# Delta-rule inversion in a hybrid decoder trunk: the running product of the squaring kept in one orientation, the other made once by transposes

## The reference, cut to what matters

```
kb = k * beta[..., None]
lower = jnp.where(strict, jnp.einsum('nbhcd,nbhmd->nbhcm', kb, k) * decay, 0.0)
a_mat = lower + jnp.eye(C, dtype=q.dtype)
rhs = jnp.concatenate([v * beta[..., None], kb * jnp.exp(gc)[..., None]], axis=-1)
sol = lax.linalg.triangular_solve(a_mat, rhs, left_side=True, lower=True)
```

## Time and profile before

| | |
|---|---|
| median of 3 runs | 2170.37 us (2168.41 to 2171.08) |
| profiled execution, its own time | 2169.47 us |
| its span, first to last instruction | 2167.6 us |
| PE busy | 2016.2 us (93%) |
| DVE busy | 1561.4 us (72%) |
| ACT busy | 1083.2 us (50%) |
| mean granted TensorE clock | 0.954 |
| the squaring, layer 0 | from 258.06 to 279.76 us |
| the squaring, layer 1 | from 913.45 to 935.15 us |

### The profile page before, as it was taken

The page is one execution under the profiler, slowest core; times in us unless marked ns, Lnnn a source line. Parts: engine busy times, 40 slices in busy tenths (PEclk is TensorE's granted clock), DMA queues, the critical chain, the costliest instruction groups (busy, mean ns, idle before and its releaser), DMA issues.

```text
span 2167.6 us, 29976 instructions
## 1 busy us (share of the span) xinstructions
PE 2016.2 (93%) x11258; PEld 1676.8 (77%) x11258; DVE 1561.4 (72%) x2174; ACT 1083.2 (50%) x1307; POOL 160.9 (7%) x245
## 2 busy tenths in 40 slices
PE   5899999989998889999979999999999999999996
PEld 2676787789998667787868878787887877888784
DVE  6582735465565483734579898999989989899996
ACT  1114221155433214221148777787777777777773
POOL 3631000000001731000000000000000000000000
PEclk9899997989999989997979999999999999999998
DMA  7465414455544345414439999999989999999992
GB/s 299 146 247 206 146 40 175 140 195 181 178 156 137 108 149 178 156 33 153 162 113 350 370 343 337 325 364 361 352 324 344 365 343 357 325 349 367 343 345 103
DMA packets 143224, 523.79 MB, mean 242 GB/s; under 512 B 17136, under 2 KB 17520, under 8 KB 142320
## 3 DMA queue, kind: packets, MB, share of 16 engines
q1 hardware_dynamic: 138960, 506.56, 65.2%
q10 hardware_dynamic: 3488, 10.07, 1.2%
q0 software_dynamic: 640, 5.35, 0.7%
HBM read 515.48 MB, written 6.43 MB: 241 GB/s over the span
## 4 chain that ended last, share of the span: by engine, by line
PE 77%; DVE 12%; POOL 4%; ACT 4%; issue 2%; DMA 1%; ACTq 0%; DVEq 0%; POOLq 0%
PE bank L859 25%; PE bank L272 14%; PE bank L885 14%; PE bank L725 10%; PE bank L429 4%; DVE wlo L1983 3%; PE bank L806 1%; DVE arena L1579 1%; ACT whi L1154 1%; PE bank L846 1%; PE bank L445 1%; PE bank L699 1%; PE bank L712 1%; PE bank L394 1%; DVE sx L1306 1%
## 5 line engine op out<-in xcount | busy, mean ns | idle before, releaser
L1983 DVE TENSOR_TENSOR wlo<-ring,whi 128x1024 fp32r<-128x1024 f32 x756 | 910.2, 1222 | 165.4 <-ACT whi L1154 159.5
L1154 ACT ACTIVATE whi<-ring 128x1024 fp32r<-128x1024 f32 x756 | 800.8, 1061 | 314.7 <-PE bank L859 150.9
L272 PE MATMUL bank<-hT,ring 128*128 128x264 f32 x1408 | 334.1, 398 | 11.6 <-issue 6.5
L272 PEld LDWEIGHTS bank<-hT,ring 128*128 128x128 f32 x1408 | 274.5, 197 | 67.4 <-issue 12.0
L859 PE MATMUL bank<-whi,gh 128*128 128x512 f32 x896 | 285.8, 400 | 3.1 <-DVE wlo L1983 2.3
L859 PE MATMUL bank<-whi,gl 128*128 128x512 f32 x896 | 279.6, 393 | 0.0
L859 PE MATMUL bank<-wlo,gh 128*128 128x512 f32 x896 | 278.7, 392 | 0.0
L859 PEld LDWEIGHTS bank<-wlo,gh 128*128 128x128 f32 x896 | 168.2, 188 | 39.1
L859 PEld LDWEIGHTS bank<-whi,gl 128*128 128x128 f32 x896 | 168.0, 188 | 37.9
L859 PEld LDWEIGHTS bank<-whi,gh 128*128 128x128 f32 x896 | 161.2, 188 | 37.0 <-DVE wlo L1983 5.7
L885 PE MATMUL bank<-whi,eh 128*128 128x512 f32 x448 | 142.3, 399 | 3.2 <-DVE wlo L1983 3.2
(11 more groups left out here) (366 smaller groups left out, 2488.5 us busy)
## 6 DMA issues: line engine op xcount, KB each, us to landing
ring<-in_w SPq DMA_DIRECT2D x964, 512.0 KB, 5.2
arena<-in_gdn ACTq DMA_DIRECT2D x2, 2048.0 KB, 8.1
out_gdns<-arena POOLq DMA_DIRECT2D x2, 2048.0 KB, 8.2
xT<-in_x ACTq DMA_DIRECT2D x1, 1056.0 KB, 11.9
out_y<-hT SPq DMA_DIRECT2D x1, 1056.0 KB, 3.9
bpk<-in_bpk ACTq DMA_DIRECT2D x2, 512.0 KB, 9.1
cpk<-in_cpk ACTq DMA_DIRECT2D x2, 512.0 KB, 9.9
bt<-in_bt ACTq DMA_DIRECT2D x2, 512.0 KB, 11.5
```

The source lines that it names most:

```text
L272: ins = pe.matmul(out, w, rhs, start=start, stop=stop)
L1154: act.activation(whi[:, m % SPL, :], ring[:, r, :], ACT.Copy).then_inc(sem("hi_done"), 1)
L1983: v.tensor_tensor(wlo[:, m % SPL, :], ring[:, (low.base + m) % RING, :], whi[:, m % SPL, :].bitcast(F32), ALU.subtract).then_inc(sem("lo_d ...
```

## The change

The product `p` is no longer kept through the three steps. Only `pT` is updated; `p` is made once, after step 2, by transposing the finished `pT` on PE (4 transposes per chunk) and copying the result from PSUM by DVE. The square `eT` of the last step is not needed either, since nothing but `p` read it, and is left out with its ACT copy. The first `p` = I + E is left out as well.

```diff
@@ PE
                         batch4(("e", l, s, c), one(at("eT", c), at("e", c)))
-                        batch4(("eT", l, s, c), one(at("e", c), at("eT", c)))
+                        if s < 2:
+                            batch4(("eT", l, s, c), one(at("e", c), at("eT", c)))
                     fill(5 + 2 * s)
                     for c in range(NC):
                         taken(pe, ("e", l, s, c))
-                        taken(pe, ("eT", l, s, c))
                         if s:
                             taken(pe, ("pT", l, s - 1, c))
-                        batch4(("p", l, s, c), one(at("eT", c), at("p", c)))
                         batch4(("pT", l, s, c), one(at("e", c), at("pT", c)))
                     fill(6 + 2 * s)
+                for c in range(NC):
+                    taken(pe, ("pT", l, 2, c))
+                    batch4(("p", l, c), lambda o, h: pe.transpose(o, mats["pT"][c][:, h, :], ident))
 
                 for s in range(3):
                     for c in range(NC):
-                        taken(pe, ("pT", l, 2, c) if s == 0 else ("xT", l, s - 1, c))
+                        taken(pe, ("p", l, c) if s == 0 else ("xT", l, s - 1, c))
@@ ACT
-                        for n in ("e", "eT"):
+                        for n in ("e", "eT") if s < 2 else ("e",):
                             name = (n, l, s, c)
-                            filled(act, ("eT", l, s, c))
+                            filled(act, ("eT" if s < 2 else "e", l, s, c))
@@ DVE
-                    tt(mats["p"][c], mats["e"][c], bc(ident[:, None, :], H4), ALU.add)
...
-                        filled(v, ("pT", l, s, c))
-                        for n in ("p", "pT"):
-                            name = (n, l, s, c)
-                            ps = filled(v, name)[:, :].rearrange("p (h t) -> p h t", h=NH)
-                            takes(v, v.tensor_tensor(mats[n][c], mats[n][c], ps, ALU.add), name)
+                        name = ("pT", l, s, c)
+                        ps = filled(v, name)[:, :].rearrange("p (h t) -> p h t", h=NH)
+                        takes(v, v.tensor_tensor(mats["pT"][c], mats["pT"][c], ps, ALU.add), name)
                     fill(6 + 2 * s)
+                for c in range(NC):
+                    name = ("p", l, c)
+                    takes(v, v.tensor_copy(mats["p"][c], filled(v, name)[:, :].rearrange("p (h t) -> p h t", h=NH)), name)
```

## The result

| | before | after |
|---|---|---|
| median | 2170.37 us (5 runs, 2167.64 to 2171.08) | 2157.28 us (5 runs, 2156.33 to 2157.92) |
| ratio | | 0.9942, 95% interval 0.9927 to 0.9956 |
| span of the profiled execution | 2167.6 us | 2155.3 us |
| start of the squaring to first `yl`, per layer | 24.03 us | 17.92 us |
| the 48 records of the first level | 7.22 us | 7.22 us |

The account below looks back on a forecast made before the run. PE's matmuls were taken to bound the squaring. Per layer 7.15 us saved less 0.77 and 0.2 gives 6.2, 12.4 for two; 2169.47 became 2157.1, moved towards the median to 2157.3 us, range 2152.8 to 2161.5.

Parts of the forecast that it names:

- Eight batches at 0.894: Squaring, per layer: six p and two eT batches go, 8 of 24, on PE's path, saving 7.15 us.
- The tail: End of squaring: last add's start to PE's yl takes 3.01 us instead of 2.24, costing 0.77 us more per layer.
- Hand-overs: Inside the squaring steps: four waits per layer for ACT's copies of e, 0.05 us each, 0.2 per layer.
- rival 2: Squaring steps: ACT's copy becomes the bound, PE waits 0.87 us at four hand-overs per layer; 2163.9 us, chance 0.08.
- DVE's two instructions ahead: Before the squaring: two removed masks-and-adds of 0.69 us per layer save nothing, hidden because PE is busy with projections.
- Banks and weights: PSUM bank round robin moves by six groups per layer and the weight ring is filled early; both costed at nothing.
- rival 3: Behind the squaring: one layer's gain is swallowed by a later wait for weights; 2163.3 us, chance 0.05.
- rival 1: First level: clock holds through the split hole, gaining 1.9 us in one layer or 3.7 in both; 2155.4 or 2153.4, chance 0.22.
- The clock at an unchanged price: First level behind PE's hole: clock falls as before, costing 1.86 us per layer, since transposes do not count as work.
- Rival 4: Squaring itself runs at the low clock, 0.50, because of new waits: 8.1 us slower per layer, 2185.7 us, chance 0.03.

Follow-up runs that it names:

- the tail alone: Kernel before with only step 2 of the squaring changed: eT and p batches left out there, p made by transposes; 2163.59 us, ratio 0.9975.

## Why the prediction was right

- **Eight batches at 0.894, all on the path.** Shown. With the tail alone and four batches less it is 2.61, the other four give 3.50, and two squares put back cost 1.74.
- **The tail.** From the last add's start to `yl` 3.01 us were laid out and 3.02 measured, against 2.24 before. The copies of `p` and the mask stand in the order that was foreseen. The transposes took longer than I said (0.66 with the drain for 0.60). For chunk 0 that disappears under the adds; for chunk 1 they end at 275.16, just when DVE is done with the first copy (274.47 + 0.69), so it costs nothing there either.
- **Hand-overs.** Forecast 0.2 us per layer. The chain has 14.74 us for 128 records; 16 batches are 14.30, and the chain of before carries 0.18 beyond its 24 batches (21.64 for 21.46), so 0.26 is the price. The margins of 0.02 us were thus not quite enough, in step 2 above all. The steps from add to add of chunk 0 show it: 269.11 - 263.69 = 5.42 for 5.36, and 3.75 for 3.58 in the last. The 5.42 is below the 5.6 that would have spoken for ACT as the bound (rival 2).
- **DVE's two instructions ahead at nothing.** Shown, by putting them back.
- **Banks and weights at nothing (rival 3).** Nothing was swallowed: layer 1 has the whole 6.11 again, and the stretch behind it takes 1222.8 us for 1222.9. (The 2163.3 of this rival and the 2153.4 of rival 1 are counted from 2157.1 and not from 2157.3, which changes nothing.)
- **The clock at an unchanged price.** The outcome was as forecast, 7.22 us in both layers, but two things in the working were wrong. The price is 1.56 us and not 1.86: six batches of a level take 5.66 at 1.00, since hand-overs between its batches belong to them, and 5.36 was the squaring's rate. This didn't enter the sum, as it was on both sides. And the reason for which the rule was taken, that transposes don't count, is refuted. Rival 1 asked the right question and had the wrong cause: the split hole is the same in kernels in which the clock fell and in two in which it held, and what goes with the outcome is where the hole lay. With two batches more per layer the forecast of the clock would have been wrong by 3.1 us; that it was right here is luck.
- **Rival 4.** The new waits did not cost the clock inside the squaring: 128 records took 14.74 us in both layers, at a granted clock of 1.00.

The forecast of 2157.3 then is the sum of right terms, with the missing cause of the last one hidden by its being the same before and after. That it met the median of 2157.28 to 0.02 us is luck: the rows were forecast to give 12.4 us and gave 12.2, the sum from the profiled execution was 2157.1 where that of the changed kernel took 2157.48, and the second measurement of the same kernel has 2157.91.

## What to carry to other kernels

Where the chain of waits runs through one engine without a break, removed instructions are worth their full pitch; lay out the new tail event by event and count the gaps at its end as carefully as the batches removed. When a batch is taken out between a producer's copy and its use, compare the copy and its hand-overs with what is left to cover them, here 0.87 under 0.894, which still cost 0.26 us per layer over four hand-overs: a margin of 0.02 is no margin. And when an experiment gives an unchanged total, read both stages on either side of the place: a cost of 1.74 us and a clock that held (1.56) cancelled each other.

## What was not expected of the hardware

- Transposes on PE kept the granted clock at 1.00 for 13.10 us by themselves, and filled a hole with the same outcome as matmuls did (5.66 us for the level). They are issued every 0.11 us (120 in 13.10), a float32 matmul of the same 128x128x128 every 0.22 (0.894 for four).
- The fall behind a hole of PE is repeatable, and depends on where the hole lies: idle times of 0.24 and 1.62 us cost 1.56 us of clock at distances of 36.8 to 36.9 and 40.4 to 40.5 us from the last return to 1.00 and nothing at 38.8, and 0.30 and 1.63 us cost nothing at 38.6 and 38.7. Both layers always had the same outcome, and the same distance to 0.1 us. What sets it is open.
- PE's idle time can be spent for this: 14 transposes that nobody reads shorten what follows by 1.56 us, in a hole where the clock fell without them.
